# Added identity products in TensorE's waits, and a new order of loads and scalings, in a two-layer SSD, attention and expert kernel

## What is computed

```
mod = silu(c) @ ada_w[i] + ada_b[i]        # shift, scale, gate of both sub-layers, for latent and context
h   = modulate(rmsnorm(x, norm1_g[i]), shift, scale)
x   = x + gate * mixer(h)                  # layer 0: bidirectional Mamba-2 scan; layer 1: differential attention
h2  = modulate(rmsnorm(x, norm2_g[i]), shift2, scale2)
x   = x + gate2 * grouped_moe(h2)          # layer 1: latent tokens only

grouped_moe: scores = sigmoid(h2 @ router_w); best of 4 groups, then the top 2 of its 4 experts
             out = sum over the chosen experts of weight * (silu(h2 @ w_gate) * (h2 @ w_up)) @ w_down
```

## Time and profile before

| | us |
|---|---|
| median of 3 runs | 1441.32 (1440.46 to 1442.62) |
| profiled execution | 1438.38 |
| its span, first to last instruction | 1436.2 |
| TensorE busy | 1265.4 (88%) |
| VectorE busy | 527.1 (37%) |
| ScalarE busy | 373.6 (26%) |
| GpSimd busy | 211.0 (15%) |
| HBM read | 344.20 MB, 250 GB/s over the span |
| mean granted TensorE clock | 0.941 |

### The profile page before, as it was taken

How to read it: one execution, slowest core, us unless ns; L and a number is a source line. 1 busy time by engine, 2 the same in 40 slices (tenths; PEclk the granted TensorE clock), 3 DMA queues, 4 the chain that set the end, 5 groups by cost and what they waited for, 6 DMA issues and landing times.

```text
span 1436.2 us, 12916 instructions
## 1 busy us (share of the span) xinstructions
PE 1265.4 (88%) x4989; PEld 585.5 (41%) x4989; DVE 527.1 (37%) x823; ACT 373.6 (26%) x706; POOL 211.0 (15%) x207
## 2 busy tenths in 40 slices
PE   4899999999998999299999993799998939987984
PEld 2344444444444445244443431344545424332421
DVE  1456655655663223611111112444338361111112
ACT  2336476666574001010000001300235110000000
POOL 1002243344343000000000002012002100000001
PEclk8999999999999999599999997799999959998997
DMA  9233667567646603769999996710000949999994
GB/s 355 74 121 117 249 220 262 197 219 261 235 163 224 248 30 132 277 218 428 428 426 427 427 423 257 283 59 0 0 15 1 371 156 394 427 426 428 427 428 192
DMA packets 76310, 360.02 MB, mean 251 GB/s; under 512 B 7465, under 2 KB 25753, under 8 KB 60881
## 3 DMA queue, kind: packets, MB, share of 16 engines
q1 hardware_dynamic: 67195, 326.47, 57.5%
q0 software_dynamic: 4672, 16.84, 3.1%
q10 hardware_dynamic: 4380, 15.86, 2.8%
HBM read 344.20 MB, written 14.95 MB: 250 GB/s over the span
## 4 chain that ended last, share of the span: by engine, by line
PE 70%; DMA 16%; DVE 7%; ACT 2%; issue 2%; SPq 1%; POOL 0%; POOLq 0%; DVEq 0%; ACTq 0%
PE psum L1529 22%; PE psum L2028 10%; PE psum L760 9%; PE psum L771 8%; DMA ring<-in_moe_w_up 6%; PE psum L1105 6%; PE psum L289 3%; DMA ring<-in_moe_w_down 3%; DMA hT<-in_moe_w_down 2%; PE psum L2077 2%; DMA ring<-in_ada_w 2%; PE psum L804 1%; PE psum L824 1%; DMA arena<-mod_d 1%; PE psum L820 1%
## 5 line engine op out<-in xcount | busy, mean ns | idle before, releaser
L1529 PE MATMUL psum<-ring,arena 128*64 128x512 f32 (+1 forms) x1344 | 410.3, 605 | 23.3 <-DMA ring<-in_moe_w_down 8.7
L1529 PEld LDWEIGHTS psum<-ring,arena 128*64 128x64 f32 (+1 forms) x1344 | 146.8, 152 | 259.0 <-issue 220.4
L760 PE MATMUL psum<-hT,ring 128*128 128x512 f32 x384 | 169.7, 596 | 0.0
L2028 PE MATMUL psum<-ring,hT 128*128 128x512 f32 x320 | 143.5, 608 | 2.2 <-ACT arena L2101 2.2
L1105 PE MATMUL psum<-ring 128*128 128x512 f32 x256 | 113.6, 602 | 2.3 <-ACT ring L919 1.3
L771 PE MATMUL psum<-hT,ring 128*128 128x512 f32 x256 | 112.5, 592 | 0.0
L760 PEld LDWEIGHTS psum<-hT,ring 128*128 128x128 f32 x384 | 71.3, 190 | 91.3 <-issue 91.3
L965 DVE SCALAR_TENSOR_TENSOR arena<-arena,cols 128x512 f32<-128x512 f32 x96 | 92.6, 965 | 3.4
L2028 PEld LDWEIGHTS psum<-ring,hT 128*128 128x128 f32 x320 | 61.9, 196 | 78.1 <-issue 77.4
L1600 ACT ACTIVATE arena<-psum 128x512 f32<-128x512 f32 x20 | 11.9, 597 | 268.9 <-PE psum L1529 268.9
L903 ACT ACTIVATE ring<-ring,dts 128x128 f32<-128x128 f32 x256 | 76.5, 387 | 0.5
(11 more groups left out here) (295 smaller groups left out, 1420.3 us busy)
## 6 DMA issues: line engine op xcount, KB each, us to landing
ring<-in_moe_w_gate SPq DMA_DIRECT2D x28, 2048.0 KB, 21.8
ring<-in_moe_w_up SPq DMA_DIRECT2D x28, 2048.0 KB, 18.5
ring<-in_moe_w_down SPq DMA_DIRECT2D x28, 2048.0 KB, 20.7
arena<-in_ada_w SPq DMA_DIRECT2D x60, 512.0 KB, 5.9
ring<-in_ssd_w_in SPq DMA_DIRECT2D x16, 1024.0 KB, 7.3
ring<-acs_d SPq DMA_DIRECT2D x16, 1024.0 KB, 6.7
ring<-in_da_w_in SPq DMA_DIRECT2D x6, 2048.0 KB, 15.4
ring<-in_ada_w SPq DMA_DIRECT2D x20, 512.0 KB, 4.8
```

What stands on the lines that cost most here:

```text
L760: mm = pe.matmul(psum[:, bank, :], w_[:, k, c0:c0 + P], hT[:, k, :], start=(k == 0), stop=(k == KD - 1))
L1529: mm = pe.matmul(psum[rows, dst, :], lhsT[:, k, rows], slot(s_, a)[:, k, part], start=(k == 0), stop=(k == a - 1))
L2028: mm = pe.matmul(psum[:, 4 + m_ % 2, :], hT[:, k, t * P:(t + 1) * P], slot(qkv_slot[n], KD)[:, k, :], start=(k == 0), stop=(k == KD - 1))
```

## The change

A helper is added, which multiplies the identity with a matrix of ones into a PSUM bank that nobody reads at that time. TensorE calls it in these places: twice 10 products between the pieces of the opening, 27 before the transposes of the last tile and 16 behind its logits in the first router, 20 and 16 at the same places of the second, 28 behind the ranks and 21 behind the one-hot products in both, and 28 in the passage. Three of them come with a wait ahead for the bank or the moment: `wo_added` 7, `out_added` 3 and `back_in[0]`. The pieces of the diff below are, in this order, of `ada_first_tensor`, `wout_tensor`, `router_tensor` (two), `att_tensor` and TensorE's main program.

```
+        def keep_busy(pe, bank, n):
+            for _ in range(n):
+                pe.matmul(psum[:, bank, 0:P], ident[:, :], ones[:, :], start=True, stop=True)
...
+                if k in (4, 6):
+                    keep_busy(pe, 6, 10)
...
+            pe.wait_ge(wo_added, 7)
+            keep_busy(pe, 4, 27)
             moe0.norm.tensor(pe, (3,))
             moe0.logits_part(pe, 2)
+            keep_busy(pe, 4, 16)
...
+                keep_busy(pe, 5, 28)
...
+                keep_busy(pe, 5, 21)
...
+            pe.wait_ge(A["out_added"], 3)
+            keep_busy(pe, 5, 20)
             moe1.norm.tensor(pe, (1,))
             moe1.logits_part(pe, 1)
+            keep_busy(pe, 5, 16)
...
+            pe.wait_ge(moe0.back_in[0], moe0.at["back_in"] + 32)
+            keep_busy(pe, 4, 28)
```

The permutation is made ahead of the index, and the two names change places in the count:

```
-        M_READY, AB_READY, IDX_READY, PERM_READY, POS_READY, W_READY = range(1, 7)
+        M_READY, AB_READY, PERM_READY, IDX_READY, POS_READY, W_READY = range(1, 7)
...
-                v.wait_ge(s["rank_mm"], at["rank_mm"] + 2)
-                v.tensor_copy(self.idx, psum[:, 6, 256:256 + G]).then_inc(s["route_done"], 1)
                 step(tt(out=self.grid, in0=self.hit, in1=outer(self.iota), op=ALU.mult))
                 step(v.tensor_reduce(out=self.permf, in_=self.grid.rearrange("p e r -> p r e"), axis=AX.X, op=ALU.add))
                 v.tensor_copy(self.perm, self.permf).then_inc(s["route_done"], 1)
+                v.wait_ge(s["rank_mm"], at["rank_mm"] + 2)
+                v.tensor_copy(self.idx, psum[:, 6, 256:256 + G]).then_inc(s["route_done"], 1)
```

In the passage ACT weighs two tiles ahead, and the attention weights wait for the gathers one by one:

```
         def between_scalar(act):
+            moe0.weigh_scalar(act, 0)
+            moe0.weigh_scalar(act, 1)
             for m in range(TT):
-                moe0.weigh_scalar(act, m)
                 norm_b.square(act, m)
+                if m + 2 < TT:
+                    moe0.weigh_scalar(act, m + 2)
...
         def att_sync(sp):
             for n in range(6):
-                if n == 1:
-                    for j in range(2):
-                        sp.wait_ge(moe0.row_stored[j], moe0.end["rows"][j])
-                if n == 2:
-                    sp.wait_ge(moe0.back_in[TT - 1], 32)
+                if n:
+                    sp.wait_ge(moe0.back_in[n - 1 if n < 3 else TT - 1], 32)
```

10 lines of the change are left out of this document (5 added, 5 removed).

## The result

The changed kernel takes 1431.13 us (median of 4, 1428.50 to 1432.86), the kernel before 1441.70 us beside it (median of 4, 1440.46 to 1442.62): a ratio of 0.994, with a 95% interval of 0.9921 to 0.996. By the medians it is 10.6 us faster, by the ratio 8.7 us (5.8 to 11.4), where 18.1 us were forecast. The predicted 1423 us is 8 us too low; the time lies inside the range given (1412 to 1433), but the gain is only about half of the forecast one. A later measurement of both gave 1429.07 beside 1439.37 (0.9928, 0.9914 to 0.9942).

The account below looks back on a forecast made before the run. TensorE's waits and slow-clock groups in opening, routers and passage were taken to bound time ahead of the weight-bound expert stages. Terms -4.0 - 7.2 - 8.1 + 1.2 = -18.1 us from 1441.3 gave 1423; 8-in-10 range 1412 to 1433.

Parts of the forecast that it names:

- Price of the added products and whether they bring the clock back: TensorE's waits: each added product costs 0.23 us at full clock, 0.45 at half, and such products bring the clock back.
- rival (d): Added products stay at 0.45 us and overrun their gaps in both routers: 28 us slower, 1469; chance 0.04.
- Opening, -4.0: Start of the kernel: earlier big loads 1.9, fourth product at full clock 1.6, L663 0.5; sum 4.0 us won.
- The 1.9 for the earlier pieces: Opening: big loads start 2.84 us sooner without four small loads; bounds 0.7 and 2.8 us, 1.9 taken.
- The 1.6 for the fourth product at the full clock: Opening: the fourth part of the modulation product falls from 3.47 us to a little over 1.9, winning 1.6.
- Passage, -8.1: Between the layers: first pair of row gathers 3.3 us sooner, VectorE and ScalarE chain 14.3 instead of 19.1 us, -4.8.
- nearly nothing: Passage: its 28 added products begin on a slow clock and earn nearly nothing, since the clock falls again.
- First router, -7.2: Held clock speeds transposes (0.9 twice), logits 1.75, one-hot products 1.75 and gate product 1.9: 7.2 us won.
- rival (b): Clock falls anyway between the groups, as logits and one-hot products are narrow: each router wins 3 to 4 us less, 1429; chance 0.14.
- the gather that now starts some 5 us sooner, while the last weights loaded ahead still move: First router: one of two small terms left out of the sum, said nearly to cancel with the rank products.
- Second router, +1.2: 3.3 and 0.7 us won up to the gather, 5.2 lost as weight loads stretch the gather to 10 us.
- Rival (a): Second router's first gather isn't held up: it wins 7.2 us instead of losing 1.2, in all -26.5, 1415; chance 0.22.

Follow-up runs that it names:

- the version with 8: Changed kernel with the index cast before the permutation and 8 added products, not 16, behind both routers' logits: 1423.59 us, ratio 0.9923 to the kernel before.
- the two traces with the index first: Changed kernel with the index cast ahead of the permutation again, run twice: 1420.87 and 1424.21 us, ratio 0.9873 to the kernel before both times.
- with products in between: The version with 8 plus an added product between every two last-tile logits products and every two one-hot products: 1424.19 us, ratio 0.9921 to the kernel before.

## Why the prediction was off

- **Price of the added products and whether they bring the clock back**: right. 0.23 us a product at the full clock, 0.45 at half. The rival (d) was rightly small.
- **Opening, -4.0**: -3.6 in the trace and 2.9 in the time of the part alone, so the size is nearly right, but not by the steps. The 1.9 for the earlier pieces has bounds of which the lower, 0.7, rests on no row; where TensorE still waits for the fourth piece it comes at 31.5 to 32.3, against 33.0 to 34.1 in the four traces with the old opening, 1.6 sooner by the means. The 1.6 for the fourth product at the full clock rests on one slow execution: in the three other traces with the old opening it ran at 1.92 us already. "ACT's issuing, about 3 us" is 8.5 to 11.6 us and not hidden: it put off the first transposes by 2.7 us and more (16.11 in place of 13.43). What saved the sum is that the pieces landed early enough for nobody to wait. The small rows came in time.
- **Passage, -8.1**: -7.3. The pair of gathers at -3.2 (forecast -3.3) and the chain at 14.9 (forecast 14.3). The chain alone was 15.8 without the added products (and 15.75 in the kernel before with the new order), so the forecast of VectorE's own work was 1.5 short. The added products there, said to earn "nearly nothing", were worth 0.9 us in it: with them the first tile's transposes take 1.04, without 1.94.
- **First router, -7.2**: -3.0 in one trace, 0.0 in the other, and by leaving its products out 2.0 in the time and nothing in the mean of four traces. Two steps failed. "At the full clock they cover their gaps and delay nobody" was a sum over full-clock prices; the 16 stood in a gap with 0.7 us to spare behind a group in which the clock often falls, which rival (b) had named, but with the price of the slow group alone and not of the products behind it. The overrun of 1.6 us took back the whole of the transposes' and logits' gain. The other was left out in half a sentence: "the gather that now starts some 5 us sooner, while the last weights loaded ahead still move" was to cancel against the rank products. It is the floor of this router: the tokens can't be there much before 26 us behind the loads' issue, however early the index is: eight traces show it, and with what is queued last held back the first gate product comes 5 us sooner in the version with 8. Of the 7.2 us only what follows the gather (2.8) and about 1 ahead of it could be won, and the 2.8 only where the clock holds: the first gate product took 7.10 us in one trace of the changed kernel and 9.91 in the other.
- **Second router, +1.2**: +6.0. The mechanism was the forecast one, and the sizes were wrong in both halves. The gather takes 11.8 us, not 10: the loads came ahead of it and not level. What was to be won ahead of it, 4.0, was 1.7, by the overrun of the 16 again. The first gate product was slow, as forecast, and a little slower than before (10.06 in place of 9.40). Rival (a), which forecast -7.2 for this router, would have got 3 to 4.4 (43.3 and 41.9 us in the two traces with the index first), for the same overrun.
- **Sum**: the profiled execution fell 8.2 us short of the forecast. The two routers alone make 9.0; opening and passage add 1.2, the projection 1.9 (chance), and expert stages and attention gave 3.4 that the forecast didn't have and for which no run here shows the cause; the rest, 0.5, lies behind TensorE's last product and outside the span.

## What to carry to other kernels

When a wait is shortened, look at what else is in the queues by then: a small gather that is issued while bulk loads still move lands when those are through, so that whoever made its index sooner has won little or nothing; hold the last loads of the queue behind it, if they have slack. Where two results are made one after the other, the one with the longer way behind it goes first, even if it has to wait for another engine, and nothing that starts bulk traffic may be released ahead of it. Filler in a wait must fit at half the clock, or stand where an overrun meets nobody. A DMA that spreads a vector over all partitions cost its queue's engine 2.2 to 6.2 us here; count that before moving one. And where a term rests on one slow group, look for that group in a second trace of the same code.

## What the runs showed of the hardware

The granted clock isn't a function of the program: the same stretch had 1.00 and 0.79 in two executions of one program, 0.83 and 0.67 in two of the other, and single groups differ by a factor of up to 1.9. Nor does it fall only where TensorE is idle or its products are narrow: in the versions with 8 products and with products in between it fell inside groups of the full added products that followed a narrow group or a wait. A forecast of one group's clock is a chance, and one trace of before may be a lucky one (its 535 to 545 was) or an unlucky one (its fourth product of the opening was, 3.47 us, 1.92 in the three other traces with the old opening). Issuing one vector spread over 128 partitions (`dt_bias`, 32 KB) held ScalarE for 2.98 to 6.17 us, the same instruction in different executions, while the issue of a plain load beside it took 0.49.
